# A different order in the first stage of a one-core encoder trunk: conditioning chunks, K tiles, weight halves and small loads

## The reference, cut to what matters

```python
sc = silu(c)                                  # 9 streams x 1024
mod = sc @ w_ada + b_ada                      # 1024 x 9216 weights
sh1, sc1, g1, ... = split(mod, 9)
hn = rmsnorm(x, norm_g[0]) * (1 + sc1) + sh1  # per stream
x = x + 0.5 * g1 * ((silu(hn @ W1g) * (hn @ W1u)) @ W2)
```

## Time and profile before

| What | us |
|---|---|
| Median of three runs | 1444.37 (1443.72 to 1444.69) |
| The profiled execution, its own time | 1445.51 |
| Span of the profiled execution | 1443.9 |
| PE busy | 1422.3 (99%) |
| DVE, ACT, POOL busy | 1014.5, 663.6, 71.5 |

### The profile page before, as it was taken

The page is one execution under the profiler, slowest core; times in us unless marked ns, Lnnn a source line. Parts: engine busy times, 40 slices in busy tenths (PEclk is TensorE's granted clock), DMA queues, the critical chain, the costliest instruction groups (busy, mean ns, idle before and its releaser), DMA issues.

```text
span 1443.9 us, 25671 instructions
## 1 busy us (share of the span) xinstructions
PE 1422.3 (99%) x10202; PEld 1372.2 (95%) x10202; DVE 1014.5 (70%) x1742; ACT 663.6 (46%) x1186; POOL 71.5 (5%) x121
## 2 busy tenths in 40 slices
PE   7999999999999999999999999999999999999998
PEld 6899999999999999999789999998999999999997
DVE  5767677676776776667886567557767676767776
ACT  5543525253435444666825453226425253444354
POOL 3100000000000130000100000004000000000001
PEclk9999999999999999999999999999999999999999
DMA  9752434444344612231362222444324233231222
GB/s 319 213 187 61 159 105 146 117 147 147 110 139 132 184 30 74 74 93 54 98 187 77 67 73 63 133 143 122 110 56 143 67 88 88 71 105 52 81 74 74
DMA packets 219564, 161.02 MB, mean 112 GB/s; under 512 B 6858, under 2 KB 204678, under 8 KB 219458
## 3 DMA queue, kind: packets, MB, share of 16 engines
q1 hardware_dynamic: 217490, 153.89, 35.7%
q0 software_dynamic: 1696, 5.56, 1.3%
q10 hardware_dynamic: 272, 0.10, 0.0%
HBM read 151.50 MB, written 8.03 MB: 110 GB/s over the span
## 4 chain that ended last, share of the span: by engine, by line
PE 92%; DVE 3%; DMA 2%; ACT 1%; POOL 1%; issue 1%; SPq 0%; DVEq 0%; ACTq 0%; POOLq 0%
PE acc L864 25%; PE acc L1196 19%; PE pC L1087 18%; PE acc L1087 14%; PE acc L1075 4%; PE pB L986 2%; PE acc L1145 2%; PE pC L1336 1%; DMA ada_raw<-in_w_ada 1%; DMA raw<-in_ffn_w 1%; PE pB L945 1%; PE pB L1321 1%; PE pC L1471 1%; PE pC L1355 1%; PE acc L881 0%
## 5 line engine op out<-in xcount | busy, mean ns | idle before, releaser
L1569 ACT ACTIVATE slot<-raw 128x512 fp32r<-128x512 f32 (+1 forms) x310 | 189.7, 616 | 239.4 <-PE acc L1196 137.8
L2142 DVE TENSOR_TENSOR slot<-raw,slot 128x512 fp32r<-128x512 f32 (+1 forms) x310 | 208.6, 677 | 53.8 <-ACT slot L1569 51.3
L1196 PE MATMUL acc<-hid_hi,slot 128*128 128x320 f32 x1240 | 238.5, 310 | 0.0
L1087 PE MATMUL pC<-hn_hi,slot 128*128 128x320 f32 x912 | 216.3, 309 | 0.0
L1196 PEld LDWEIGHTS acc<-hid_hi,slot 128*128 128x128 f32 x1240 | 195.1, 188 | 2.9 <-issue 2.1
L864 PE MATMUL acc<-hn_hi,whi 128*128 128x320 f32 x672 | 161.5, 322 | 0.0
L1087 PEld LDWEIGHTS pC<-hn_hi,slot 128*128 128x128 f32 x912 | 156.2, 188 | 2.5 <-issue 2.5
L864 PE MATMUL acc<-hn_hi,wlo 128*128 128x320 f32 x672 | 153.5, 310 | 0.0
L864 PE MATMUL acc<-hn_lo,whi 128*128 128x320 f32 x672 | 153.5, 310 | 0.0
L1087 PE MATMUL acc<-tT,slot 128*128 128x320 f32 x912 | 146.3, 309 | 0.0
L1196 PE MATMUL acc<-hid_lo,slot 128*128 128x320 f32 x620 | 142.0, 308 | 0.0
(11 more groups left out here) (389 smaller groups left out, 2404.3 us busy)
## 6 DMA issues: line engine op xcount, KB each, us to landing
raw<-in_ffn_w SPq DMA_DIRECT2D x86, 512.0 KB, 5.1
sraw<-in_w_ada SPq DMA_DIRECT2D x26, 1024.0 KB, 7.2
wraw<-in_w_in SPq DMA_DIRECT2D x36, 512.0 KB, 3.6
raw<-in_ffn_w SPq DMA_DIRECT2D x16, 1024.0 KB, 5.0
ada_raw<-in_w_ada SPq DMA_DIRECT2D x8, 1024.0 KB, 11.0
wraw<-in_w_out SPq DMA_DIRECT2D x16, 512.0 KB, 4.2
raw<-in_ffn_w SPq DMA_DIRECT2D x8, 768.0 KB, 4.4
sraw<-in_w_ada_final SPq DMA_DIRECT2D x6, 1024.0 KB, 7.5
```

The lines of the kernel that those rows point to most:

```text
L1087: last = mm(out, w[:, kk * P:(kk + 1) * P], a, start=(first and kk == 0 and t == 0), stop=(kk == KQ - 1 and t == 2), skip_group_check=not ...
L1196: last = mm(a[h], w[t // 2][:, k, :], (hid_hi, hid_lo)[t % 2][:, k * TOK + h * HALF:k * TOK + (h + 1) * HALF], start=(k == 0 and t == 0), ...
L1569: A(slot_as(fi, b, 0), source_of(fi, b), ACT.Copy).then_inc(blk_hi, 1)
L2142: V.tensor_tensor(out=slot_as(fi, b, 1), in0=source_of(fi, b), in1=slot_as(fi, b, 0).bitcast(F32), op=ALU.subtract).then_inc(blk_lo, 1)
```

## The change

Five things are changed in the first stage. The two `c_row` loads are issued on ACT's queue instead of SP's. The K tiles are taken in their natural order, and the chunks in the order that belongs to it. The second weight half is loaded behind chunk 5 instead of chunk 3, and its blocks 2 and 3 are made in front of tile position 4 instead of 2. The matmuls of chunk 6 stand in front of tile position 4 and those of chunk 7, with the columns of 6 and 7, in front of position 5; the matmuls of chunk 0 stand ahead of `spread_r`. The sample tokens of the tiles at even positions are multiplied, scaled and shifted on DVE (`times_r` over all 640 tokens and the new `first_samples`), and POOL keeps those at odd positions.

```diff
-FIRST_CHUNK = (0, 4, 2, 6, 1, 5, 3, 7)
+FIRST_CHUNK = (0, 4, 1, 5, 2, 6, 3, 7)
-FIRST_TILE = (0, 1, 4, 5, 2, 3, 6, 7)
-FIRST_ROWS = {0: (0, 1), 1: (2, 3), 2: (4,), 3: (5,), 4: (6, 7)}
-FIRST_COLS = {0: (0, 1), 1: (2, 3), 3: (4, 5), 4: (6, 7)}
+FIRST_TILE = tuple(range(KD))
+FIRST_ROWS = {0: (1,), 1: (2, 3), 2: (4,), 3: (5,), 4: (6,), 5: (7,)}
+FIRST_COLS = {0: (0, 1), 1: (2, 3), 3: (4, 5), 5: (6, 7)}
@@ SP @@
-        sp.dma_start(c_row[0:1, :], c_prompt).then_inc(c_in, 16)
-        sp.dma_start(c_row[1:NSTR, :], c_sample).then_inc(c_in, 16)
...
         load_first_weights(0)
-        for s in range(2, 4):
+        for s in range(2, 6):
             load_first(s)
         load_first_weights(1)
-        for s in range(4, ADA_FIRST):
+        for s in range(6, ADA_FIRST):
             load_first(s)
@@ POOL, norm_samples @@
-                first_product(0)
                 first_product(1)
+                first_product(3)
...
                 if m == 0:
+                    if j % 2 == 0:
+                        continue
                     pool.wait_ge(mod_ready, j // 2 + 1)
+                    pool.wait_ge(tms_ready, j)
...
-                    if j + 2 < KD:
-                        first_product(j + 2)
+                    if j + 4 < KD:
+                        first_product(j + 4)
@@ PE @@
+        pe.wait_ge(c_used, 1)
+        first_rows(0)
         pe.wait_ge(xt_done, TT)
         spread_r(0)
-        pe.wait_ge(c_used, 1)
@@ ACT, norm_first @@
-            blk(0, 2)
-            blk(0, 3)
             for j in range(2, KD, 2):
+                if j == KQ:
+                    blk(0, 2)
+                    blk(0, 3)
...
+        act.dma_start(c_row[0:1, :], c_prompt).then_inc(c_in, 16)
+        act.dma_start(c_row[1:NSTR, :], c_sample).then_inc(c_in, 16)
         act.wait_ge(c_in, 32)
@@ DVE @@
+        def first_samples(j):
+            f = FIRST_TILE[j]
+            tv = by_stream(hn_f(f)[:, SEQ:TOK])
+            scale, shift = (modc[:, q + f, 1:NSTR].unsqueeze(2).broadcast_to([P, DEC_BATCH, DEC_SEQ]) for q in (KD, 0))
+            dve.wait_ge(prod_ready, j + 1)
+            st.done(V.tensor_tensor(out=tv, in0=tv, in1=scale, op=ALU.mult))
+            wait(dve, tms_ready, j)
+            V.tensor_tensor(out=tv, in0=tv, in1=shift, op=ALU.add).then_inc(tms_ready, 1)
...
-            for f in FIRST_TILE[0:KQ]:
-                times_r(f, SEQ)
+            for j in range(KQ):
+                times_r(FIRST_TILE[j], SEQ if j % 2 else TOK)
             first_scale(0)
+            first_samples(0)
...
             for j in range(2, KD, 2):
                 first_scale(j // 2)
-                if j == 2:
+                first_samples(j)
+                if j == KQ:
                     blk(0, 2)
                 low(j, FIRST_TILE[j])
-                if j == 2:
+                if j == KQ:
                     blk(0, 3)
```

More of the change, by code:

```diff
@@ L946, in to_tokens, with cond_rows, chunk_cols, first_rows @@
             return last
+        def cond_rows(bank, raw):
+            for k in range(KD):
+                q = k % (P // QUAD)
+                last = mm(ch_rows[bank][q * QUAD:(q + 1) * QUAD, :], c_f32[:, k, :], kxn(raw, KD, ADA_COLS)[:, k, :],
+                          start=(k < P // QUAD), stop=(k >= KD - P // QUAD))
+            last.then_inc(ch_mm, 1)
+        def chunk_cols(i, m, bank, row):
+            pe.wait_ge(ch_row, i + (m + 1))
+            for f in range(2):
+                last = mm(ch_cols[bank][:, f * NSTR:(f + 1) * NSTR], row[:, f * P:(f + 1) * P], quadsum[:, 0:NSTR],
+                          start=True, stop=True)
+            last.then_inc(ch_tr, 1)
+        def first_rows(s):
+            wait(pe, ch_row, s - 1)
+            pe.wait_ge(ada_in[FIRST_RAW[s]], 16 * (1 + FIRST_RAW[:s].count(FIRST_RAW[s])))
+            cond_rows(s % 2, ada_raw[FIRST_RAW[s]])
         pe.wait_ge(pool_step, 2)
@@ L999, in duo_cols @@
             last.then_inc(d_tr, 1)
-        def cond_rows(bank, raw):
-            for k in range(KD):
-                q = k % (P // QUAD)
-                last = mm(ch_rows[bank][q * QUAD:(q + 1) * QUAD, :], c_f32[:, k, :], kxn(raw, KD, ADA_COLS)[:, k, :],
-                          start=(k < P // QUAD), stop=(k >= KD - P // QUAD))
-            last.then_inc(ch_mm, 1)
-        def chunk_cols(i, m, bank, row):
-            pe.wait_ge(ch_row, i + (m + 1))
-            for f in range(2):
-                last = mm(ch_cols[bank][:, f * NSTR:(f + 1) * NSTR], row[:, f * P:(f + 1) * P], quadsum[:, 0:NSTR],
-                          start=True, stop=True)
-            last.then_inc(ch_tr, 1)
-        def first_rows(s):
-            wait(pe, ch_row, s - 1)
-            pe.wait_ge(ada_in[FIRST_RAW[s]], 16 * (1 + FIRST_RAW[:s].count(FIRST_RAW[s])))
-            cond_rows(s % 2, ada_raw[FIRST_RAW[s]])
         def first_cols(s):
@@ L2176, in norm_first @@
             low(1, FIRST_TILE[1])
-            for f in FIRST_TILE[KQ:KD]:
-                times_r(f, SEQ)
+            for j in range(KQ, KD):
+                times_r(FIRST_TILE[j], SEQ if j % 2 else TOK)
             for j in range(2, KD, 2):
                 first_scale(j // 2)
-                if j == 2:
+                first_samples(j)
+                if j == KQ:
                     blk(0, 2)
                 low(j, FIRST_TILE[j])
-                if j == 2:
+                if j == KQ:
                     blk(0, 3)
```

## The result

The changed kernel took 1446.84 us (median of 22 runs, 1445.14 to 1447.80) against 1444.36 us (22 runs, 1442.82 to 1447.10) for the kernel before, measured side by side. The ratio is 1.0015, with a 95% interval of 1.0009 to 1.0022. It is 2.5 us slower. That is outside the range predicted (1443.0 to 1445.3), and on the other side of no change. It is still within 0.2% of no change, though near its edge.

What follows compares the result with a forecast made beforehand. The prediction took the first stage to be bound by the full DMA pipe up to 39.99, then by a chain through ACT to pair 1. Terms of -0.21 and -0.18 summed to -0.39, giving 1444.0 us; range 1443.0 to 1445.3.

Steps and rivals of the forecast that it cites:

- What bounds the kernel: First stage: the full DMA pipe up to 39.99, then a chain through ACT's gate to pair 1 at 49.95.
- The landing of c_row: Start of the kernel: the small loads, issued on ACT beside SP's x issues, land about 0.3 late.
- d: Lateness of c_row from issuing on ACT: taken as 0.3, between nothing and 1.14.
- third rival: c_row is served behind x on the DMA engines, 5 late; kernel 4.3 slower, 1448.7; chance 0.04.
- second rival: c_row is late by 0.7 to 3, gain used up at 0.69; at 1.14 the kernel takes 1444.8; chance 0.25.
- the locked generator: Issues of SP and ACT would take turns, putting c_row some 0.9 late and turning the sum to +0.2.
- d is paid in full: Everything up to the first K tile hangs on c_row, so its lateness counts there in full.
- From tile 0 to chunk 7: PE's terms sum to 16.89; chunk 7's matmuls start at 39.92 against 40.13, 0.21 earlier.
- On time within 0.1: Tile 0: DVE's weight lows slip by 0.6, yet the first low part, due 1.15 into the tile, is on time.
- Samples on DVE: Before tile 0: the high part starts at 21.95 instead of 22.68 behind POOL, 0.73 earlier.
- Tile 4 out of the tail: Behind chunk 7: PE has 1.76 less to do, which wins nothing because pair 1 waits for ACT's gate.
- The sum: -0.21 at chunk 7 and -0.18 behind it make -0.39; the median goes from 1444.37 to 1444.0.

Runs made afterwards that it cites:

- e13: e11 with the two c_row loads on ACT's queue, as in the change; 1447.19 us (1 run).
- e3: The changed kernel, but SP issues the x loads only once c_row has landed; 1444.58 us (1 run).
- e11: e7 with DVE making tile 0's low part ahead of the second weight low part; 1443.72 us against 1444.14 for the kernel before, ratio 0.9997.
- e6: The kernel before with only ACT's gate moved ahead of two weight copies; 1444.53 us (1 run).
- e2: The kernel before with only the two c_row loads moved to ACT's queue; 1445.55 us against 1444.56 for the kernel before, ratio 1.0006.
- e12: e8 with all sample tokens back on POOL, as in the kernel before; 1445.05 us (1 run).
- e4: e1 with chunk 7's matmuls and the columns of 6 and 7 again ahead of tile position 4; 1444.22 us (1 run).
- e7: e5 with ACT's table load ahead of chunk 7's row copy and seven clock-keeping matmuls; 1443.64 us against 1444.40 for the kernel before, ratio 0.9998.
- e1: The changed kernel with the two c_row loads back at the head of SP's queue; 1445.06 us against 1444.56 for the kernel before, ratio 0.9999.
- e5: e1 with ACT's gate ahead of two weight copies; 1443.91 us against 1444.40 for the kernel before, ratio 0.9999.
- e14: The same kernel as e1, run once more without any edit; 1445.43 us (1 run).
- e8: e1 with seven instead of four clock-keeping matmuls ahead of tile 0; 1444.72 us against 1444.40 for the kernel before, ratio 1.0002.

## Why the prediction was wrong

**What bounds the kernel.** Right in the main. The start of pair 1 set the time: the 1.96 there is the 1.96 at the next waited transfer and 2.12 further on, and the medians differ by 2.48. "What pair 1 gains, the kernel gains" left out that the transfer behind it lands 8.3 to 10.7 after its issue. Both profiles compared here have PE's wait for it, while eight of the 14 do not; e13 has it at 1.21. How much of the 0.4 between 2.12 and 2.48 comes from a more frequent or longer wait there is not shown.

**The landing of c_row: the step that failed.** I took the lateness d as 0.3, with bounds of 0 and 1.14; it was 1.74. I had worked out both bounds from the lengths of issues, as if the lateness could only arise in the issuing. The issues were indeed only 0.16 behind. The lateness came from the transfer, 3.41 instead of 1.83, because the eight packets of the samples' load now begin behind packets of x, at 3.75 instead of 2.25. I had named this mechanism in the third rival, but as all or nothing, at 5 us, the median landing of a whole x tile. A lateness of 1.74 lies inside the second rival's condition (0.7 to 3), which I had priced only at its bound from the issues, 1.14. e3 shows the cause (3.40 with x held back, 4.94 beside it), e13 against e11 the price (1.92 at chunk 7 for 1.62 of c_row and 0.31 of turn).

The Trainium skill (DMA: Bandwidth & Descriptors, "Issuing engines are not separate DMA queues") says that transfers run on the same 16 engines whoever starts them, and interleave. By that page the move could win nothing but issue time on SP's sequencer, and the landing was open to x's packets; e3 agrees. The rule that I did weigh, the locked generator (Perfetto Trace Analysis, "DMA Instruction — HWDGE (DVE, Sync)"), gave some 0.9 for d. The trace does not bear it out: the two issues took 0.82 in all beside SP's, and the same 0.81 in e3 while SP issued nothing.

**d is paid in full.** Right, and it is why the miss counts. Before the change the pipe pinned chunk 7 near 40: a turn longer by 0.80 moved it by only 0.13 (e6), and even 2.67 were paid only with 1.40 at pair 1 (e2). After the change nothing pins it. The second bet that I lost lies here too: I took the turn as the 12.77 of the one profile of before, which is the shortest of the 14 executions (up to 13.71). The changed kernel had 13.25, which is 0.48 of its loss: 19 slow matmuls at the start of PE's turning of x instead of 12. I gave this no term since I did not know it varied. It is not shown that the change has a part in it; with `c_row` on SP the turn lay between 12.77 and 13.71 too.

**From tile 0 to chunk 7.** Predicted 16.89, measured 17.26. The whole 0.37 is tile 0: 2.42 instead of 1.96, less 0.09 in the other terms. "On time within 0.1" was wrong for the first low part. I had pushed DVE's weight lows by 0.6 but not the low part behind them. e11 shows that reordering does not help, and e12 that the samples are the cause (1.96 without them).

**Right within 0.1:** x issued at 0.94. Chunk 0's matmuls ahead of `spread_r` at no cost (they fit into DVE's work). Samples on DVE, 0.73 predicted and 0.69 measured up to tile 0 (the reciprocal is 2.23 late, tile 0 1.54; 0.69 in e12 too). The wait for chunk 4 gone and the second weight half hidden. The high part at position 6 waits for its shift and no longer for POOL, 0.18 predicted and 0.17 measured from chunk 7 to pair 1 (9.82 to 9.65). Pair 1 released by ACT's gate with more than 1 us of idle PE, 1.45.

**Tile 4 out of the tail.** I said that it wins nothing by itself, and asked only whether the transfer or PE would be last at chunk 7. I did not ask what the same tile costs in front of a chain that ends in ACT. e4 shows it: 0.5 lost.

**The sum.** Of the 2.35 between the pair 1 predicted (49.56) and measured (51.91), 1.44 is d, 0.48 the turn, 0.37 tile 0, and the rest rounding. The case that came is the second rival (a chance of 0.25), with a cause that I had given only to the third. By my own sum a d of 1.74 gives -0.69 + 1.74 = +1.05, 1445.4, already outside the range; the turn and tile 0 add 0.85, 1446.3. The range ended at the near part of the second rival, because the bound of d left the transfer out.

**A version that does better.** e7 and e11 keep the change's new order, put `c_row` back on SP, fill ACT's waiting with the table load, put the gate first and have seven matmuls ahead of tile 0 instead of four. Pair 1 starts at 49.34 and 49.19. Their medians are 3.2 and 3.1 below the changed kernel's, in other batches, and their ratios to the kernel before end at 1.0007 and 1.0006, where the changed kernel's begins at 1.0009. Against the kernel before they are 0.8 and 0.4 lower, with intervals that hold 1. So they are better than the changed kernel, and not shown to be better than the kernel before.

## What to carry to other kernels

A small load that everything waits for belongs at the head of the queue that carries the large ones: moved to a queue of its own it is issued hardly later, but its packets begin behind theirs instead of ahead of them. When a change takes a stage off a full pipe, the pipe's wait had also been the cover of everything ahead of it, so price each small lateness again without that cover, and take its bounds from landings, not from issues. And before a wait is filled with useful work, compare the work's length with the wait's: here 1.96 in a wait of 1.38 pushed back a chain on another engine. Last, one profile of the kernel before is one draw: here its turn was the shortest of 14, and it had both the wait near 100 us and the fall near 620 us.

## What the runs showed of the hardware

- A load of 32 KB took 1.83 from its issue to its landing ahead of the 512 KB loads in the same queue, 1.89 from ACT's queue with SP silent (e3, 1.50 to 3.39), and 3.41 beside 512 KB loads of the other queue. Its packets began 0.9, 0.9 and 2.3 after the issue and took under 0.4 each. ACT's first issue in the program took 0.52 with or without SP issuing beside it, against 0.34 on SP.
- The granted clock fell to 0.50 (1.2 GHz, the lower of the two levels) for 3.4 us in two executions (e1, e5), some 1.7 into the matmuls that followed an idle stretch of 1.8, and not in e14, e4 or the changed kernel, with the same idle time at the same place. In e1 it cost 1.6 at pair 1. With more matmuls in that idle time (e7, e8, e11, e12, e13) no profile shows it.
- PE busy without a gap is no protection: in the profiles of before, e1 and e14 the clock stood at 0.88 to 0.95 in 610 to 630 us with PE busy 100%, and at 1.00 there in the changed kernel's, e5's and e8's. It cost 1.5 in the profile of before (the shift against the changed kernel goes from 2.11 to 0.59).
- The turn of c and x (from ACT's start on `c_row` to the reciprocal) varied by 0.94 between executions, half as much as the whole effect at pair 1. It follows the number of matmuls, 12 to 26 of 40, that PE makes at half pace before it speeds up. What sets that moment stays open, and so does what sets off the clock's falls.
- The same 1 MB transfer, issued behind the same work near 85 us, landed 8.3 to 9.0 after its issue in eight executions and 10.0 to 10.7 in six. What decides it stays open.
